# Both MLP products as seven products of block sums for eight, on 512x512 weight quarters

## Chip, cores and metric

One NeuronCore of a Trainium2 chip runs the kernel. The metric is device time in microseconds (us), lower is better, as the median of several executions. TensorE multiplies, VectorE and ScalarE read its PSUM banks and prepare operands, GpSimd does small vector work, and SyncE (SP) issues the DMA transfers.

## Reference

One inference step of a two-layer encoder over 640 token rows: 512 rows of one prompt (tiles 0 to 3 of 128 rows) and 8 streams of 16 rows (the sample tile, number 4). `D_MODEL` is 1024, `D_FF` 4096. Each layer mixes tokens (retention heads and a short convolution on a common input projection) and then applies the MLP:

```python
x = x + jnp.concatenate([ret_out, conv_out], axis=-1) @ w_out
h2 = rms_norm(x, ln2_w)
x = x + jnp.square(jax.nn.relu(h2 @ w_up)) @ w_down     # (640x1024)(1024x4096), (640x4096)(4096x1024)
```

All of it is float32. A final RMS norm gives the outputs.

## The kernel before

**Split products.** A float32 product is three passes of the TensorE format fp32r: every operand is split into a high part (ScalarE copies it into an fp32r tile) and a low part (VectorE subtracts the high part from the raw value), and high x high, high x low and low x high are accumulated in PSUM. Weights are split on the chip: a unit of 128x2048 values (1 MB) comes by DMA into `w_raw`, goes to `w_hi` on ScalarE (line 685) and to `w_lo` on VectorE (line 1046).

**Order.** Every engine has its own queue written out in program order, and semaphores count between them. In a layer come the mixer stages K, V, Q, G, C, H, B, the output projection O in two column halves of five tiles, and then the MLP. During O's second half each finished tile is normalised into `xn`, transposed by TensorE (a turn "n2": four 128x128 transposes per half; two turns, a turn pair, per tile) and split into `norm_hi` and `norm_lo`, which hold the tokens transposed (features on the partitions). Turn n2 of the last tile stands inside the first up block. The turn pair of the next layer's first norm ("n1", 0) stands inside the last down block of layer 1.

**MLP.** The hidden width is cut into 8 blocks of 512. `up_block` makes 8 groups (4 column tiles x 2 halves of 320 tokens), each 8 k-tiles x 3 passes of matmuls with 320 moving columns (line 479); ScalarE takes the relu, VectorE squares it, ScalarE and VectorE split it into `inner_hi` and `inner_lo`. `down_block` makes 10 groups (2 column halves x 5 token tiles) of 4 k-tiles x 3 passes with 512 columns (line 469), and VectorE adds each into `x` (line 1313). Up block b+1 runs before down block b, and weights have two buffers (`par`), so that splits run a whole chunk ahead. Six banks take the groups in turn.

**Engines beside TensorE.** GpSimd forms the reciprocal root of each row's mean square from ScalarE's sum of squares (line 929), which VectorE's `normalise` (line 1065) waits for.

Of the kernel before, what the change touches and what calls it, by code (L numbers as in the profile page):

```python
# [25 lines left out]
NBLK = 4 * D // 512  # L26
# [4 lines left out]
ORDER = [SAMPLE, 0, 1, 2, 3]  # L31

# [7 lines left out]
          + [("O", dh, t) for dh in range(2) for t in range(NT)])  # L40
# [3 lines left out]
                                  ("B", 0, 0), ("O", 0, 0), ("O", 1, 0))]  # L44
MIX_CHUNKS = len(STAGE_START)
UPS, DOWNS = 2 * FT, 2 * NT
PER_BLOCK = UPS + DOWNS
PER_LAYER = MIX + NBLK * PER_BLOCK
CHUNKS = MIX_CHUNKS + 2 * NBLK
# [5 lines left out]
SCALAR_PER_LAYER = len(MIX_SCALAR) + NBLK * UPS  # L55
VECTOR_PER_LAYER = len(MIX_VECTOR) + NBLK * DOWNS

# [15 lines left out]
SPLIT_TURNS = [n for n, x in enumerate(TURNS) if x[0] in ("n1", "n2", "o")]  # L73


def split_turns_to(n):
# [20 lines left out]
              **{("O", 1, t): [("n2", t - 1, 0), ("n2", t - 1, 1)] for t in range(1, NT)}}  # L97
# [3 lines left out]
def up_group(b, j):  # L101

    if isinstance(b, int) and b == 0:
        return MIX + j
    return b * PER_BLOCK + (MIX + UPS - PER_BLOCK + j)


def down_group(d, j):
    if isinstance(d, int) and d == NBLK - 1:
        return PER_LAYER - DOWNS + j  # L110
    return d * PER_BLOCK + (MIX + 2 * UPS + j)


def up_chunk(b):
    return MIX_CHUNKS if isinstance(b, int) and b == 0 else b * 2 + (MIX_CHUNKS - 1)


def down_chunk(d):
    return CHUNKS - 1 if isinstance(d, int) and d == NBLK - 1 else d * 2 + (MIX_CHUNKS + 2)


def parity_up(b_is_first):
    return MIX_CHUNKS % 2 if b_is_first else (MIX_CHUNKS + 1) % 2


def parity_down(d_is_last):
    return (CHUNKS - 1) % 2 if d_is_last else (MIX_CHUNKS + 2) % 2


def program(nc, x_p, x_s, state_ret, state_conv, norm_rows, ln2_w, w_in, conv_w, ret_w, w_out, w_up, w_down,  # L130
# [6 lines left out]
    with ctx:  # L137
# [17 lines left out]
        norm_hi = place("norm_hi", [P, KT, TOK], f32r)  # L155
        norm_lo = place("norm_lo", [P, KT, TOK], f32r)
        w_hi = place("w_hi", [P, 2, 2, 4, 512], f32r)
        w_lo = place("w_lo", [P, 2, 2, 4, 512], f32r)
        w_raw = place("w_raw", [P, 2, 4, 512], f32)


# [15 lines left out]


# [4 lines left out]
        relu = place("relu", [P, 4, HALF], f32, vo_at)  # L183
# [13 lines left out]

        norm_row = place("norm_row", [P, D], f32)
        ret_row = place("ret_row", [P, RW], f32)
        ret_state = place("ret_state", [P, H, HD], f32)  # L200
# [30 lines left out]
        mlp_bank = mix_bank + small_bank  # L231
# [23 lines left out]
        group_done = Signal("group_done", PER_LAYER, start=1)  # L255
        turned = Signal("turned", len(TURNS))
# [26 lines left out]
        squared = Signal("squared", NBLK * UPS)  # L283
        hidden_hi = Signal("hidden_hi", NBLK * UPS)
        hidden_lo = Signal("hidden_lo", NBLK * UPS)
# [34 lines left out]
        def _(sp):  # L320
            for_w_in = w_in.rearrange("l (a k p) (s c) -> l s a p k c", a=2, p=P, c=512)
            for_w_out = w_out.rearrange("l (a k p) (s c) -> l s a p k c", a=2, p=P, c=512)
            for_up = w_up.rearrange("l (a k p) (s c) -> l s a p k c", a=2, p=P, c=512)
            for_down = w_down.rearrange("l (s k p) (a c) -> l s a p k c", k=4, p=P, c=512)
# [34 lines left out]
            with sp.Fori(0, DEPTH) as layer:  # L359
# [4 lines left out]

                sp.dma_start(ret_row[:], ret_w[bass.ds(layer, 1), :].to_broadcast([P, RW])).then_inc(
# [3 lines left out]

                sp.wait_ge(group_done.sem, group_done.at(layer, 0))  # L370
# [33 lines left out]
                units(up_chunk(0), for_up, 0)  # L404
                with sp.Fori(0, NBLK // 2 - 1) as turn:
                    for b in range(2):
                        units(up_chunk(turn * 2 + (b + 1)), for_up, turn * 2 + (b + 1))
                        units(down_chunk(turn * 2 + b), for_down, turn * 2 + b)
# [271 lines left out]
        def _(act):  # L680
# [69 lines left out]
            with act.Fori(0, DEPTH) as layer:  # L750
# [6 lines left out]
                for p in range(2, NT):  # L757
                    square1(layer, p)
                    if p == NT - 1:
                        split_unit(layer, 1, 0, 1, 0)  # L760
# [668 lines left out]
```

## Time and profile before

| | |
|---|---|
| median of 3 runs | 1497.02 us (1496.27 to 1497.89) |
| profiled execution, span from its first to its last instruction | 1495.1 us |
| the same execution's own time, outside the span included | not listed apart; the three runs lie 1.2 to 2.8 us above the span |
| TensorE matmul busy | 1480.4 us (99%), 8326 instructions |
| TensorE weight loads busy | 1336.0 us (89%) |
| VectorE busy | 651.8 us (44%) |
| ScalarE busy | 393.8 us (26%) |
| GpSimd busy | 126.3 us (8%) |
| granted TensorE clock, mean | 0.998 of full speed |
| read from HBM | 115.83 MB, 82 GB/s over the span with what is written |

Busy time of TensorE is the union of overlapping matmuls, so it shows where there are gaps and not how fast the matmuls follow each other. A wait is printed in square brackets behind an instruction, with the engine that released it.

### The profile page before, as it was taken

Reading aid. Unit: us, or ns where it says so; the run is one execution under the profiler, and the core shown is the slowest. Engines: PE = TensorE matmul, PEld = TensorE weight load, DVE = VectorE, ACT = ScalarE, POOL = GpSimd, SP = SyncE. Lnnn points to the kernel's source line nnn. Section 1 sums busy time; section 2 is a strip of 40 time slices with the busy share of each in tenths; the row PEclk is TensorE's granted clock in tenths of the full one; section 3 lists DMA queues with packets and bytes.
Section 4 is the critical chain, followed back from the end, with each engine's and each line's share of the span. In section 5 each row is a group of like instructions: output and inputs, shape, how many; then the busy total and the mean of one; then the engine's idle time right before and its main releaser. Section 6 shows DMA issues by size and latency. Waiting matters only on the chain.

```text
span 1495.1 us, 21805 instructions
## 1 busy us (share of the span) xinstructions
PE 1480.4 (99%) x8326; PEld 1336.0 (89%) x8326; DVE 651.8 (44%) x970; ACT 393.8 (26%) x579; POOL 126.3 (8%) x153
## 2 busy tenths in 40 slices
PE   7999999999999999999999999999999999999998
PEld 6888999899989989989888889988999899889886
DVE  5346435355334334334362562444543433433433
ACT  5212222233123222222142203213422223223121
POOL 2343100000000000000033330000000000000000
PEclk9999999999999999999999999999999999999999
DMA  7323112122212213213042231221131221221301
GB/s 257 128 85 114 64 57 84 59 85 82 89 57 93 75 56 108 74 57 120 1 133 80 85 114 64 78 94 57 62 109 57 84 85 56 90 93 56 106 8 71
DMA packets 74643, 124.27 MB, mean 83 GB/s; under 512 B 3332, under 2 KB 20868, under 8 KB 74568
## 3 DMA queue, kind: packets, MB, share of 16 engines
q1 hardware_dynamic: 74424, 123.18, 24.9%
q8 instruction: 50, 0.82, 0.2%
q14 instruction: 25, 0.20, 0.0%
q10 hardware_dynamic: 144, 0.07, 0.0%
HBM read 115.83 MB, written 7.41 MB: 82 GB/s over the span
## 4 chain that ended last, share of the span: by engine, by line
PE 99%; DVE 0%; ACT 0%; DMA 0%; issue 0%; POOL 0%; DVEq 0%; POOLq 0%; ACTq 0%
PE bank L469 51%; PE bank L479 41%; PE bank L519 2%; PE bank L557 1%; PE bank L564 1%; PE bank L538 1%; PE bank L542 0%; PE bank L547 0%; PE bank L550 0%; DMA x<-in_x_sample 0%; PE bank L555 0%; DVE norm_lo L1089 0%; DVE w_lo L1054 0%; DVE xn L1065 0%; ACT L691 0%
## 5 line engine op out<-in xcount | busy, mean ns | idle before, releaser
L479 PE MATMUL bank<-norm_hi,w_hi 128*128 128x320 f32 x1408 | 436.1, 310 | 0.0
L479 PE MATMUL bank<-norm_hi,w_lo 128*128 128x320 f32 x1408 | 435.3, 309 | 0.0
L479 PE MATMUL bank<-norm_lo,w_hi 128*128 128x320 f32 x1408 | 435.3, 309 | 0.0
L469 PE MATMUL bank<-w_hi,inner_hi 128*128 128x512 f32 x800 | 312.1, 390 | 0.0
L469 PE MATMUL bank<-w_lo,inner_hi 128*128 128x512 f32 x800 | 311.6, 389 | 0.0
L469 PE MATMUL bank<-w_hi,inner_lo 128*128 128x512 f32 x800 | 311.5, 389 | 0.0
L685 ACT ACTIVATE w_hi<-w_raw 128x2048 fp32r<-128x2048 f32 x96 | 178.7, 1907 | 350.1 <-PE bank L469 322.4
L479 PEld LDWEIGHTS bank<-norm_hi,w_hi 128*128 128x128 f32 x1408 | 264.4, 188 | 0.6
L479 PEld LDWEIGHTS bank<-norm_lo,w_hi 128*128 128x128 f32 x1408 | 264.4, 188 | 0.5
L479 PEld LDWEIGHTS bank<-norm_hi,w_lo 128*128 128x128 f32 x1408 | 264.4, 188 | 0.0
L1313 DVE TENSOR_TENSOR x<-x,bank 128x512 f32<-128x512 f32 x180 | 123.6, 687 | 293.9 <-PE bank L469 293.9
L1046 DVE TENSOR_TENSOR w_lo<-w_raw,w_hi 128x2048 fp32r<-128x2048 f32 (+1 forms) x100 | 219.7, 2201 | 5.5 <-ACT w_hi L685 5.5
L1345 DVE TENSOR_TENSOR relu<-relu 128x320 f32<-128x320 f32 x128 | 63.0, 492 | 265.6 <-ACT relu L880 265.6
L469 PEld LDWEIGHTS bank<-w_hi,inner_lo 128*128 128x128 f32 x800 | 150.2, 188 | 31.3
L469 PEld LDWEIGHTS bank<-w_lo,inner_hi 128*128 128x128 f32 x800 | 150.2, 188 | 30.4
L469 PEld LDWEIGHTS bank<-w_hi,inner_hi 128*128 128x128 f32 x800 | 150.2, 188 | 30.4
L469 PE MATMUL bank<-w_hi,norm_hi 128*128 128x512 f32 x320 | 129.1, 404 | 2.5 <-DVE w_lo L1054 2.5
L880 ACT ACTIVATE relu<-bank 128x320 f32<-128x320 f32 x128 | 55.6, 436 | 282.5 <-PE bank L479 282.5
L469 PE MATMUL bank<-w_hi,norm_lo 128*128 128x512 f32 x320 | 125.7, 393 | 0.0
L469 PE MATMUL bank<-w_lo,norm_hi 128*128 128x512 f32 x320 | 125.5, 392 | 0.0
L926 POOL TENSOR_SCALAR var<-sums 128x1 f32<-128x1 f32 x25 | 4.8, 191 | 1196.7 <-ACT xn L703 1191.0
L469 PEld LDWEIGHTS bank<-w_hi,norm_hi 128*128 128x128 f32 x320 | 60.5, 189 | 15.2 <-ACT w_hi L691 2.9
(104 smaller groups left out, 918.1 us busy)
## 6 DMA issues: line engine op xcount, KB each, us to landing
w_raw<-in_w_mlp_up SPq DMA_DIRECT2D x32, 1024.0 KB, 5.4
w_raw<-in_w_mlp_down SPq DMA_DIRECT2D x32, 1024.0 KB, 5.0
w_raw<-in_w_in SPq DMA_DIRECT2D x28, 1024.0 KB, 5.1
w_raw<-in_w_out SPq DMA_DIRECT2D x8, 1024.0 KB, 5.0
past_state<-in_state_ret SPq DMA_DIRECT2D x8, 512.0 KB, 4.1
out_ret_s<-past_state SPq DMA_DIRECT2D x8, 512.0 KB, 4.9
x<-in_x_prompt SPq DMA_DIRECT2D x4, 512.0 KB, 12.4
norm_row<-in_norm_rows SPq DMA_DIRECT2D x3, 512.0 KB, 5.6
```

The lines of the kernel that those rows point to most:

```text
L469: mm = pe.matmul(out, act[a][:, k, tile * P:(tile + 1) * P], w_of(b, n), start=(n == 0 and m == 0), stop=(n == len(ks) - 1 and m == 2))
L479: mm = pe.matmul(out, ws[a][:, par, k // 4, k % 4, ft * P:(ft + 1) * P], norms[b][:, k, half * HALF:(half + 1) * HALF], start=(k == 0 and ...
L519: mm = pe.transpose(out[:, i * P:(i + 1) * P], src[i], identity)
L538: mm = pe.matmul(out[:, h * P:(h + 1) * P], kT[:, ORDER[p], h], qT, start=True, stop=True)
L557: mm = pe.matmul(out[:, 0:HD], q_spread[:, b], past_state[h % 2][:, b], start=False, stop=(b == NB - 1))
L564: mm = pe.matmul(out[:], k_rot[:, SAMPLE, h * HD:(h + 1) * HD], v_spread[:, 4 * c:4 * c + 4], start=True, stop=True)
L685: nc.scalar.activation(w_hi[:, par, half], w_raw[:, half], ACT.Copy).then_inc(w_hi_ready.sem, 1)
L880: nc.scalar.activation(relu[:, j % 4], mlp_bank[slot % 6][:, 0:HALF], ACT.Relu).then_inc(scalar_read.sem, 1)
L926: nc.gpsimd.tensor_scalar(tmp, src, scale, eps, ALU.mult, ALU.add).then_inc(eps_step.sem, 1)
L1046: ins = nc.vector.tensor_tensor(w_lo[:, par, half, ks], w_raw[:, half, ks], f(w_hi[:, par, half, ks]), ALU.subtract)
L1313: nc.vector.tensor_tensor(xx, xx, src[:], ALU.add).then_inc(vector_read.sem, 1)
L1345: nc.vector.tensor_tensor(relu[:, j % 4], relu[:, j % 4], relu[:, j % 4], ALU.mult).then_inc(squared.sem, 1)
```

## The change

Both MLP products are done by Strassen's method (in Winograd's form of block sums) for the four prompt tiles. The hidden width is cut into 4 blocks (`NBLK`) of 1024. A block is two quads of weights, one for up and one for down; a quad is a 1024x1024 matrix in four quarters of 512x512, named 11, 12, 21, 22. The prompt side is cut into 2x2 as well: 256 tokens x 512 features. Seven products of sums take the place of eight; the code calls them B11, B21, SUM_1112, SUM_111222, SUM_1222, B22, SUM_ALL, and the text counts them as products 1 to 7 in this order. Products 1, 2 and 6 use a quarter as it is; the other four use sums that VectorE forms in place in the raw quarters. The sample tile stays plain: it uses the four stored quarters' worth of items (products 1, 2, 5, 6: `SAMPLE_PART`) in groups of 12 matmuls with 512 columns and the tokens as the stationary operand, so its hidden values come out by rows and are turned back (`turn_sample`).

Up products have 256 moving columns, where there were 320. Weights are split by halves of an item (128x1024) into a ring of two items. The turn of tiles is ordered 0, 1, sample, 2, 3 (`OUT_ORDER`), and the last two turn pairs of a layer's norm stand inside the first up block. The differences of the normalised input are made in the first block, those of the hidden values in each block. PE here is TensorE, dve VectorE, act ScalarE.

```diff
-NBLK = 4 * D // 512
+NBLK = 4 * D // 1024
+PRODUCTS = 7
+B11, B21, SUM_1112, SUM_111222, SUM_1222, B22, SUM_ALL = range(PRODUCTS)
+SAMPLE_PART = {B11: 0, B21: 1, SUM_1222: 0, B22: 2}
...
+def half_used(item, h):
+    quad, i = divmod(item, PRODUCTS)
+    b = quad // 2
+    if quad % 2 == 0:
+        return STEP["up sample", b, i] if i in (B11, B21, B22) else STEP["up", b, i, h]
+    return STEP["down sample", b, i] if i in (B11, B21) else STEP["down", b, i, h, 1]
...
@@ SP @@
+                for quad in range(1, QUADS):
+                    first = (quad - 1) * PRODUCTS
+                    sp.wait_ge(weights_summed.sem, weights_summed.at(layer, sums_to(quad - 1, SUM_ALL, 1)))
+                    load_quarter(layer, quad, "11")
+                    sp.wait_ge(half_lo.sem, half_lo.at(layer, 2 * (first + SUM_1222) + 2))
+                    load_quarter(layer, quad, "21")
+                    sp.wait_ge(half_lo.sem, half_lo.at(layer, 2 * (first + B22) + 2))
+                    load_quarter(layer, quad, "12")
+                    sp.wait_ge(half_lo.sem, half_lo.at(layer, 2 * (first + SUM_ALL) + 2))
+                    load_quarter(layer, quad, "22")
@@ PE @@
+                def up_half(b, i, h, chain, other):
+                    item = 2 * b * PRODUCTS + i
+                    wait_item(item, h)
+                    out = {B21: other, SUM_1112: bank_c, B22: bank_c}.get(i, chain)[h]
+                    for n in range(2):
+                        cols = out[:, n * 256:(n + 1) * 256]
+                        for k in range(4):
+                            for m, (a, c) in enumerate(three):
+                                mm = pe.matmul(cols, item_half(item, h, a)[:, k, n * P:(n + 1) * P],
+                                               mlp_in[i][c][:, k], ...)
+                    mm.then_inc(step_done.sem, 1)
...
+                def up_sample(b, i):
+                    item = 2 * b * PRODUCTS + i
+                    wait_item(item, 1)
...
+                    for k in range(4):
+                        for m, (a, c) in enumerate(three):
+                            mm = pe.matmul(out, x5[a][:, k], w[c][:, :, k], ...)
...
+                def down_piece(b, i, h, pair):
+                    item = (2 * b + 1) * PRODUCTS + i
+                    wait_item(item, h)
+                    out = {B21: bank_b, SUM_1112: bank_c, B22: bank_c}.get(i, bank_a)[pair]
+                    a_item = a_ring[:, (b * PRODUCTS + i) % 2]
+                    for k in range(2):
+                        for m, (a, c) in enumerate(three):
+                            mm = pe.matmul(out[:], a_item[:, a, 2 * h + k, pair * P:(pair + 1) * P],
+                                           item_half(item, h, c)[:, k], ...)
...
+                def down(b):
+                    for i in range(PRODUCTS):
+                        if i == SUM_1222:
+                            pe.wait_ge(x_added.sem, x_added.at(layer, x_adds_to(b, B21, "sample")))
+                        if i in (SUM_1222, B22):
+                            down_sample(b, i)
...
@@ ScalarE @@
+                def weight_half(item, h):
...
+                        act.wait_ge(step_done.sem, step_done.at(layer, half_used(item - 2, h) + 1))
+                    nc.scalar.activation(item_half(item, h, 0), raw_half(quad, RAW_OF[i], h), ACT.Copy
+                                         ).then_inc(half_hi.sem, 1)
@@ VectorE, the queue of one block; lines with "if b == 0" are the first block's @@
+                def up(b):
+                    q, item = 2 * b, 2 * b * PRODUCTS
...
+                    weight_half(item + 2, 1)
+                    weight_sum(q, SUM_111222, 0)
+                    if b == 0:
+                        in_difference(0)
+                        in_difference(1)
+                    hidden_sum(b, B21, 0)
+                    weight_half(item + 3, 0)
+                    hidden_sum(b, B21, 1)
+                    weight_sum(q, SUM_111222, 1)
+                    if b == 0:
+                        in_diff_lo_of(1)
+                        in_difference(2)
+                    weight_half(item + 3, 1)
+                    weight_sum(q, SUM_1222, 0)
+                    if b == 0:
+                        in_diff_lo_of(2)
+                    weight_half(item + 4, 0)
+                    weight_sum(q, SUM_1222, 1)
+                    if b == 0:
+                        in_diff_lo_of(3)
+                        in_diff_lo_of(4)
+                    sample_lo(b, 0)
+                    weight_half(item + 4, 1)
...
+                def down(b):
+                    q, item = 2 * b + 1, (2 * b + 1) * PRODUCTS
+                    weight_sum(q, SUM_1112, 0)
+                    weight_half(item + 1, 1)
+                    a_difference(b, SUM_1112)
+                    sample_lo(b, 2)
+                    weight_half(item + 2, 0)
+                    a_difference(b, SUM_1222)
+                    for p in range(2):
+                        add_to_x(b, B11, p)
+                    weight_sum(q, SUM_1112, 1)
+                    a_item_lo(b, SUM_1112)
+                    weight_sum(q, SUM_111222, 0)
+                    weight_half(item + 2, 1)
+                    a_difference(b, SUM_111222)
+                    weight_half(item + 3, 0)
+                    for p in range(2):
+                        add_to_x(b, B21, p)
+                    add_to_x(b, B21, "sample")
+                    weight_sum(q, SUM_111222, 1)
+                    a_item_lo(b, SUM_111222)
+                    weight_half(item + 3, 1)
+                    weight_sum(q, SUM_1222, 0)
+                    a_difference(b, B22)
+                    weight_half(item + 4, 0)
+                    for p in range(2):
+                        add_to_x(b, SUM_1112, p)
+                    weight_sum(q, SUM_1222, 1)
+                    a_item_lo(b, SUM_1222)
+                    weight_half(item + 4, 1)
...
```

In the down quad the same names hold with item numbers 7 higher; the hidden values' own split items (`a_item_hi` on ScalarE, `a_item_lo` on VectorE) have a ring of two as well. The hidden values are kept in four f32 quarters, into which ScalarE copies three of the products and VectorE adds the others (`hidden_sum`), before ScalarE's relu and square.

## Rows read from the trace of the kernel before

**Rows 1.** Page, the chain that ended last: shares of the span by line.
```profile
PE bank L469 51%; PE bank L479 41%; PE bank L519 2%; PE bank L557 1%; PE bank L564 1%; PE bank L538 1%; PE bank L542 0%; PE bank L547 0%; PE bank L550 0%; DMA x<-in_x_sample 0%; PE bank L555 0%; DVE norm_lo L1089 0%; DVE w_lo L1054 0%; DVE xn L1065 0%; ACT L691 0%
```

**Rows 2.** Timeline, TensorE, 320 columns: start, duration (us), engine, line, operation, tiles, shapes.
```profile
306.55 0.31 PE L479 MATMUL bank<-norm_lo,w_hi 128*128 128x320 f32 x1
...
313.30 0.31 PE L479 MATMUL bank<-norm_hi,w_lo 128*128 128x320 f32 x1
```

**Rows 3.** Timeline, TensorE, down or O products of 512 columns.
```profile
300.31 0.40 PE L469 MATMUL bank<-w_lo,inner_hi 128*128 128x512 f32 x1
...
305.30 0.39 PE L469 MATMUL bank<-w_hi,inner_lo 128*128 128x512 f32 x1
```

**Rows 4.** Both MLPs by windows: length, busy us (instructions) by engine, clock, DMA share, GB/s.
```profile
306.32:751.23 444.91, 444.91 (x2515) 407.30 (x2514) 186.55 (x251) 114.81 (x174) 2.19 (x6) 1.00 0.22 73
1044.12:1488.12 444.00, 444.00 (x2507) 406.27 (x2505) 184.07 (x246) 113.83 (x172) 3.30 (x10) 1.00 0.21 70
```

**Rows 5.** Timeline, TensorE, transposes and plain f32 passes, and what follows each.
```profile
99.44 1.95 PE L557 MATMUL bank<-past_state,q_spread 128*128 128x128 f32 x16
...
101.22 1.88 PE L564 MATMUL bank<-v_spread,k_rot 128*128 128x512 f32 x4
...
305.53 1.03 PE L519 MATMUL bank<-const,xn 128*128 128x128 f32 x8
306.32 0.39 PE L479 MATMUL bank<-norm_hi,w_hi 128*128 128x320 f32 x1
```

**Rows 6.** Groups of instructions, shapes apart: count, busy us, mean ns, idle before.
```profile
L1065 DVE SCALAR_TENSOR_TENSOR xn<-x,rstd,norm_row 128x1024 f32<-128x1024 f32 x22 | 28.2, 1284 | 27.4 <-POOL rstd L929 27.3
...
L703 ACT ACTIVATE xn<-x 128x1024 f32<-128x1024 f32 x22 | 23.3, 1061 | 84.9 <-DVE x L1313 82.3 <-DMA x<-in_x_sample 2.6
L732 ACT ACTIVATE norm_hi<-bank 128x512 fp32r<-128x512 f32 x40 | 21.6, 589 | 38.3 <-PE bank L519 38.3
...
L1046 DVE TENSOR_TENSOR w_lo<-w_raw,w_hi 128x1024 fp32r<-128x1024 f32 x8 | 9.8, 1219 | 0.0
```

**Rows 7.** Timeline, VectorE, two instructions back to back.
```profile
758.14 1.29 DVE L1065 SCALAR_TENSOR_TENSOR xn<-x,rstd,norm_row 128x1024 f32<-128x1024 f32 x1
759.34 0.68 DVE L1106 TENSOR_TENSOR k_rot<-bank,const 128x512 f32<-128x512 f32 x1
```

**Rows 8.** Timeline, handoffs: ScalarE to VectorE, TensorE to ScalarE, VectorE to TensorE.
```profile
453.56 0.44 ACT L880 ACTIVATE relu<-bank 128x320 f32<-128x320 f32 x1 [3.06 <-PE bank L479]
...
454.03 0.49 DVE L1345 TENSOR_TENSOR relu<-relu 128x320 f32<-128x320 f32 x1 [0.81 <-ACT relu L880]
...
470.70 0.31 PE L479 MATMUL bank<-norm_hi,w_lo 128*128 128x320 f32 x1
...
471.05 0.44 ACT L880 ACTIVATE relu<-bank 128x320 f32<-128x320 f32 x1 [2.72 <-PE bank L479]
...
754.52 2.50 DVE L1054 TENSOR_TENSOR w_lo<-w_raw,w_hi 128x512 fp32r<-128x512 f32 x4 [2.40 <-ACT w_hi L691]
...
755.36 0.47 PE L469 MATMUL bank<-w_hi,norm_hi 128*128 128x512 f32 x1 [0.36 <-DVE w_lo L1054]
```

**Rows 9.** Timeline, the end: ScalarE sum, GpSimd between, VectorE.
```profile
1490.00 0.19 ACT L911 ACTIVATION_READ_ACCUMULATOR squares_out<-x 128x1 f32 x1
...
1491.23 1.42 DVE L1075 SCALAR_TENSOR_TENSOR x<-x,rstd,norm_row 128x512 f32<-128x512 f32 x2 [1.03 <-POOL rstd L929]
```

**Rows 10.** DMA issues of up weights: KB each, median us to landing.
```profile
w_raw<-in_w_mlp_up SPq DMA_DIRECT2D x32, 1024.0 KB, 5.4
```

**Rows 11.** Timeline, TensorE near the start: idle before a matmul.
```profile
12.64 0.47 PE L469 MATMUL bank<-w_hi,norm_hi 128*128 128x512 f32 x1 [2.10 <-DVE w_lo L1054]
```

**Rows 12.** Windows of 2 us at the start; the clock stands before the DMA share.
```profile
12.00:14.00 2.00, 1.36 (x5) 1.20 (x6) 2.00 (x4) 2.00 (x4) 0.00 (x0) 0.90 1.08 420
14.00:16.00 2.00, 2.00 (x6) 1.56 (x5) 0.96 (x2) 1.97 (x4) 1.44 (x3) 0.50 1.00 401
16.00:18.00 2.00, 2.00 (x12) 1.58 (x12) 2.00 (x4) 2.00 (x5) 0.20 (x1) 0.74 1.01 403
```

More of the change, by code:

```diff
@@ L96 @@
               ("B", 0, 0): [("tail",)],
[L97 to L115, printed above, removed]
@@ L118, in down_chunk @@
[L118 to L127, printed above, removed]
+              **{("O", 1, OUT_ORDER[p + 2]): [("n2", p, 0), ("n2", p, 1)] for p in range(3)}}
+PRODUCTS = 7
+B11, B21, SUM_1112, SUM_111222, SUM_1222, B22, SUM_ALL = range(PRODUCTS)
+SAMPLE_PART = {B11: 0, B21: 1, SUM_1222: 0, B22: 2}
@@ new lines, in mlp_steps @@
+def mlp_steps():
+    out = []
+    for b in range(NBLK):
+        for i in range(PRODUCTS):
+            if i == SUM_1222:
+                out.append(("up sample", b, i))
+            out.append(("up", b, i, 0))
+            if i == SUM_ALL:
+                out.append(("turn sample", b, 1))
+            out.append(("up", b, i, 1))
+            if i in (B11, B21, B22):
+                out.append(("up sample", b, i))
+            if i == SUM_1112:
+                out.append(("turn sample", b, 0))
+        for i in range(PRODUCTS):
+            if i in (SUM_1222, B22):
+                out.append(("down sample", b, i))
+            out += [("down", b, i, h, pair) for h in range(2) for pair in range(2)]
+            if i in (B11, B21):
+                out.append(("down sample", b, i))
+    return out
@@ L471, in tokens_product, with features_product @@
                 return mm
-            def features_product(out, ft, half, par, before=None):
+            def features_product(out, ft, half, chunk, before=None):
                 for k in range(KT):
@@ new lines, in up_sample @@
+                def up_sample(b, i):
+                    item = 2 * b * PRODUCTS + i
+                    wait_item(item, 1)
+                    out = sample_bank[:].rearrange("p (h c) -> p h c", h=2)
+                    w = [item_part(item, part).rearrange("p (h k c) -> p h k c", h=2, k=4) for part in range(2)]
+                    x5 = sample_in[SAMPLE_PART[i]]
+                    for k in range(4):
+                        for m, (a, c) in enumerate(three):
+                            mm = pe.matmul(out, x5[a][:, k], w[c][:, :, k],
+                                           start=(i in (B11, SUM_1222) and (k, m) == (0, 0)),
+                                           stop=(k == 3 and m == 2), skip_group_check=True)
+                    mm.then_inc(step_done.sem, 1)
@@ new lines, in down_sample @@
+                def down_sample(b, i):
+                    item = (2 * b + 1) * PRODUCTS + i
+                    wait_item(item, 1)
+                    part = SAMPLE_PART[i]
+                    pe.wait_ge(mid_lo.sem, mid_lo.at(layer, 3 * b + part + 1))
+                    for k in range(4):
+                        for m, (a, c) in enumerate(three):
+                            mm = pe.matmul(sample_bank[:], sample_mid[part][a][:, k],
+                                           item_half(item, k // 2, c)[:, k % 2],
+                                           start=(i in (B11, SUM_1222) and (k, m) == (0, 0)),
+                                           stop=(k == 3 and m == 2), skip_group_check=True)
+                    mm.then_inc(step_done.sem, 1)
@@ L1375, in _ @@
[L1375 to L1382 removed]
+                            read_turn_lo(layer, ("n2", p - 2, c))
@@ new lines, in _ @@
+                for b in range(NBLK):
+                    up(b)
+                    down(b)
+                with dve.If(layer < DEPTH - 1):
+                    split_first(layer + 1, 0)
+                for p in range(2):
+                    normalise(layer + 1, 0, p, ORDER[p], 16)
+                with dve.If(layer < DEPTH - 1):
+                    for c in range(2):
+                        read_turn_lo(layer + 1, ("n1", 0, c))
+                with dve.If(layer > DEPTH - 2):
+                    normalise_last(2)
@@ L1385, in _ @@
+                for p in range(2):
+                    add_to_x(NBLK - 1, SUM_ALL, p)
             normalise_last(3)
```

868 lines of the change are left out of this document (647 added, 221 removed).

## Prediction, made before the change was run

> **What bounds the kernel now.** I read the chain that ended last first: nearly all of it is matmuls of lines 469 and 479, so every microsecond is TensorE's, and the next question is what one matmul costs [rows 1]. A matmul's printed duration overlaps the next, so the price is start to start. At 320 columns it is (313.30 - 306.55)/46 = 0.1467 us [rows 2]; at 512 it is (305.30 - 300.31)/22 = 0.2268 us [rows 3]. Both are columns/2.4 GHz plus 13.4 ns (133.3 + 13.4; 213.3 + 13.4). The stretches by layer come next: from the first up matmul to the last down matmul 444.9 and 444.0 us, VectorE busy 187 and 184, ScalarE 115 and 114, the clock 1.00 [rows 4]. My prices give 1536 x 0.1467 + 960 x 0.2268 = 443.0 us, plus 1.0 for each turn pair, eight transposes at 0.1 and a slower matmul behind them [rows 5], of which layer 1 has two and layer 2 one: 445.0 and 444.0. So the MLPs run without a gap.
>
> **What TensorE gains.** A block is now 1024 hidden columns, four per layer. Up: 7 products x 48 matmuls of 256 columns, 4 sample groups x 12 of 512, and two sample transposes. Down: 7 x 24 and 4 x 12 of 512. The trace has no 256-column matmul. Below it stands the plain f32 pass, 128 columns with a weight load each, at (101.22 - 99.44)/16 = 0.111 us; above it the 320 columns' 0.147. I take 256/2.4 + 13.4 = 0.120, the line through both measured widths [rows 2, 3, 5]. Block: 40.3 + 10.9 + 1.0 (0.5 for four transposes and the change of width) + 38.1 + 10.9 = 101.2 us. Eight are 810; with two turn pairs in each first block and one at the first layer's end, 815. Before: 889, plus one turn pair per layer that the O stage no longer holds, 891. TensorE alone: **-76 us**.
>
> The Trainium skill (TensorE: Matmul & The Clock Gate, "Back-to-back issue gap") gives columns/2.4 + 2.5 ns, thus an estimate of 0.109 us at 256 and about 21 us less than my sum. The trace doesn't agree: the same rule gives 0.136 and 0.216 where the rows have 0.147 and 0.227 [rows 2, 3].
>
> **What VectorE and ScalarE must add.** A half item is 128x1024: VectorE 1.22 us, the next one starting 0.08 sooner, so 1.14 in a row; a 512 operation 0.68, so 0.61; a 1024 scalar_tensor_tensor 1.20; ScalarE's 1024 pass 1.05; its 512 copy 0.6 [rows 6, 7]. VectorE per block: 28 splits, 16 weight sums, 7 activation splits and 2 differences at 1.14 (60), 2 differences at 1.20 (2), 26 half-width operations (6 hidden sums, 16 adds to x, 4 for the sample) at 0.61 (16): 79 us of 101. ScalarE has 54. So neither is full on average; what counts is where the queue is full. Handoffs: 0.04 from a matmul's end to its reader (0.20 after TensorE's next start), 0.03 from ScalarE to VectorE, the same taken back, 0.15 from VectorE to a waiting matmul [rows 8].
>
> I walk one steady block (t=0 at its first matmul; products 1 to 7 in the code's order).
>
> *Stall 1, product 5 of up.* The weight ring holds two items, so item 4 may be split only when TensorE has left item 2's, its sample group included: t = 17.0 (4 x 2.88 + 2 x 2.72). Then in VectorE's order: ScalarE's half (0.20 + 1.05 + 0.03), split 1.14, hidden sum 0.61, weight sum 1.22, ScalarE 1.12, split 1.14, sum 1.22, ScalarE 1.12, split 1.14, sum 1.22, ScalarE 1.12, split 1.22, 0.15. Product 5 opens with the sample group, which needs both halves, so it starts at 30.7. TensorE needs only products 3 and 4 and a transpose, to 29.0. **1.7 us.** The sums sit between the ScalarE passes because the next half is copied out of the sum just made.
>
> *Stalls 2 and 3, products 4 and 5 of down.* From 30.7 TensorE needs 31.5 us to leave down's product 1 and its sample group: 62.2. Nothing of item 3's first half can be made earlier (same ring slot); ScalarE hands it over at 63.5. From there VectorE's queue has no gap. Ahead of product 4's activation split (a_item_lo) stand 8 operations of 1.14 (three weight splits, three weight sums, a difference, product 3's activation split), five adds to x (3.05) and a difference of 1.20; with itself (1.22) and 0.15 they end at 78.2. TensorE has done products 2 and 3 at 75.8 (5.4 + 2.7 + 5.4): **2.4 us.** Product 4 takes 5.4, to 83.6. VectorE goes on from 78.0 with a split, sum, difference (1.20), split, two adds, sum, activation split and at last the second half of product 5's weights, which its sample group wants: 5 x 1.14 + 1.20 + 2 x 0.61 + 1.22 + 0.15, thus 87.5. **3.9 us**, and 0.2 for the add to x of product 4 that still holds product 5's bank. Queued behind each are the adds to x and the splits of the next item; those keep up, being 1 us or more ahead of need. From 87.5 TensorE has 21.8 of work: the block ends at 109.5 where without waits it would at 101.3: **8.2 us each, 66 for eight**.
>
> *First block.* Five splits and three differences of the normalised input join VectorE's queue. With them the ScalarE passes of stall 1's chain find VectorE busy: from t = 20.4 it has 9 operations of 1.14 (three of them such splits), three of 0.61, one difference of 1.20 and the last split of 1.22 in a row, 14.5 us, so product 5 starts at 35.1 where TensorE, with its 2.0 of norm transposes, is ready at 31.0: 4.1 instead of 1.7, **5 us** for both layers.
>
> *End of layer 1.* The next norm's chain starts only after product 6's last piece (104.0): 0.2, ScalarE's four 512 pieces 2.2, the square 1.06 + 0.18 [rows 6, 9], 1.04 from its sum through GpSimd to VectorE's normalise [rows 9], 1.3 for that: the transposes start at 110.1 where TensorE is ready at 108.2, and with K's first product waiting 0.3 for the low part it is **2 us** in all. The end of the kernel keeps its order and its tail.
>
> *Moved or free.* Transfers: as many of 1 MB as before, landing 5.4 us after issue [rows 10]. The tightest is quarter 11 of the next up: issued after the seventh weight sum (91.8), there at 97, used at 101. It costs nothing with 4 us in hand; without them its lateness would be paid one for one, behind it quarters 21, 12 and 22 on SP's queue, the latter two needed later than the next block's start. The four quarters of the first block are queued at the O stage's second half, 30 us ahead. The mixer only has other addresses; the two splits of item 0 inside the O stage stand ahead of VectorE's add and normalise but fit a 5.4 us group.
>
> **Sum.** -76 + 66 + 5 + 2 = -3 us. The profiled execution's span is 1495.1, so 1491.8; the runs' median lies 1.9 above that span, so **1494 us**. A small difference of two large terms, then: TensorE gives back nearly all of an eighth of its products while waiting for VectorE.
>
> **Rivals.**
> 1. *The clock falls in the stalls* (slower). After 2.1 us of idle ahead of 12.64, and short ones before, the granted clock was 0.90, 0.50 and 0.74 in the next three 2 us windows, the lower level of 1.2 GHz; its price there is the missing share, 2 x (0.10 + 0.50 + 0.26) = 1.7 us [rows 11, 12]. Stall 3 is longer than that idle, and the sample group behind it is on the path. Against it: matmuls surround the stall, where the early stretch was sparse. One fall per block: +14, 1508; two, stall 2 as well: +27, 1521. Two falls in the kernel decide.
> 2. *256 columns go at 0.111* (faster): 240 of a block's 336 such matmuls are on the path (products 1, 2, 5, 6, 7; 3 and 4 hide under VectorE's chain): 8 x 240 x 0.0087 = -17: 1477. For: the f32 pass bears a weight load at that pace [rows 5]. Against: the constant 13.4 of both fp32r widths. The skill's rule above goes this way.
> 3. *The weight load is the floor at 0.147*: products 1 and 2 +2.6, 3 and 4 then longer than VectorE's chain by 0.8, 5 to 7 +3.8: 7.2 a block, +57: 1551. Against: 0.111 and the transposes' 0.1 have loads too.
> 4. *VectorE keeps ahead, no stalls in the blocks*: -76 + 2: 1423. It needs 6 us off the 24 us of queue ahead of stall 3, a quarter off each operation; the rows by form allow no such thing [rows 6].
>
> **Chances.** My forecast 0.45 (own range 1486 to 1502: the prices to 2% and the handoffs to 0.1 us), clock 0.24, pace down 0.12, pace up 0.07, no stalls 0.12 (my walk could be wrong in an order). 0.2% is 3 us, about what this measurement can tell from no change. The forecast's 0.45 splits 0.24 faster, 0.15 same, 0.06 slower: faster 0.48, same 0.15, slower 0.37. The range leaves out pace up and no stalls, 0.19: 1473 to 1521.
>
> **What the new profile would show.** 256-column matmuls 0.120 apart; TensorE idle before product 5's sample group in up (about 1.7), product 4 (2.4) and product 5's sample group in down (3.9), each released by VectorE's low parts; VectorE about 640 us busy in the MLPs, 0 idle between down's product 1 and product 5; blocks of 109 us; clock 1.00. A clock under 1.00 after stall 3, starts 0.111 or 0.147 apart, or a TensorE idle only at layer ends each name their rival. Most fragile: the walk's order of halves, since 1 us per block is 8 in the sum.

## Result, and the profile after

The changed kernel takes **1519.87 us** (median of 4 runs, 1517.21 to 1522.83) where the kernel before took 1497.45 (4 runs beside it): ratio 1.015, 95% interval 1.0132 to 1.0168, so 1.5% slower. The forecast was 1494, 0.2% faster. The four runs lie in two pairs, 1517.2 and 1517.3 against 1522.4 and 1522.8; the profile is of the first, so a difference to this kernel's median is good to some 3 us either way. The profiled execution has a span of 1515.4 us where before has 1495.1, and a mean granted clock of 0.979 where before has 0.998.

The page of the changed kernel: busy time by engine, then the chain that ended last by engine.

```profile
PE 1433.9 (95%) x8198; PEld 1265.7 (84%) x8198; DVE 947.2 (63%) x1152; ACT 593.2 (39%) x743; POOL 131.6 (9%) x153
...
PE 77%; DVE 12%; issue 6%; ACT 4%; POOL 0%; DVEq 0%; DMA 0%; ACTq 0%; POOLq 0%
```

Where [rows 1] had TensorE's two matmul lines with 92% of the chain, VectorE now holds 12% and ScalarE 4%. What TensorE waits for (total us, times, longest):

```profile
PE bank L876 <- DVE ring L1775: 25.2, 8, 3.6
PE bank L784 <- DVE ring L1775: 18.7, 8, 4.0
PE bank L863 <- DVE a_ring L1840: 17.5, 8, 2.2
```

These are the three stalls of the prediction (waits of TensorE inside a block), each eight times: L876 is product 5's sample group in down (stall 3), L784 its sample group in up (stall 1), L863 product 4 of down (stall 2), all released by VectorE. Nothing else waits inside the blocks. The price of a 256-column matmul, from the first and the last start of a product in the timeline of TensorE:

```profile
421.10 0.28 PE L770 MATMUL bank<-mlp_in_hi,ring 128*128 128x256 f32 x1
...
426.85 0.63 PE L784 MATMUL bank<-ring,sample_in_hi 128*128 128x512 f32 x2
```

Product 1 has 48 matmuls: 5.75/48 = 0.120 us each, the value taken. Now down in the second and third block, where a group's start shows the stall before it:

```profile
499.28 7.35 PE L863 MATMUL bank<-ring,a_ring 128*128 128x512 f32 x24 [2.19 <-DVE a_ring L1840]
508.56 0.74 PE L876 MATMUL bank<-ring,sample_mid_hi 128*128 128x512 f32 x2 [1.93 <-DVE ring L1775]
...
610.41 5.73 PE L863 MATMUL bank<-ring,a_ring 128*128 128x512 f32 x24 [2.19 <-DVE a_ring L1840]
619.70 1.22 PE L876 MATMUL bank<-ring,sample_mid_hi 128*128 128x512 f32 x2 [3.56 <-DVE ring L1775]
```

and the windows of the second block's stretch (the clock stands before the DMA share):

```profile
497.00:499.00 2.00, 0.09 (x1) 0.00 (x0) 2.00 (x2) 1.05 (x1) 0.00 (x0) 1.00 0.00 0
499.00:501.00 2.00, 1.72 (x5) 1.39 (x6) 2.00 (x3) 0.01 (x1) 0.00 (x0) 0.67 0.00 0
501.00:503.00 2.00, 2.00 (x7) 1.52 (x6) 1.94 (x3) 1.49 (x2) 0.00 (x0) 0.50 0.00 0
503.00:505.00 2.00, 2.00 (x10) 1.65 (x9) 2.00 (x4) 0.52 (x1) 0.00 (x0) 0.97 0.00 0
...
507.00:509.00 2.00, 0.44 (x2) 0.39 (x3) 2.00 (x3) 2.00 (x3) 0.00 (x0) 1.00 0.00 0
509.00:511.00 2.00, 2.00 (x8) 1.57 (x7) 2.00 (x3) 1.09 (x2) 0.00 (x0) 0.73 0.00 0
511.00:513.00 2.00, 2.00 (x6) 1.59 (x5) 2.00 (x3) 0.00 (x0) 0.00 (x0) 0.50 0.00 0
513.00:515.00 2.00, 2.00 (x9) 1.61 (x9) 2.00 (x3) 0.00 (x0) 0.00 (x0) 0.91 0.26 40
```

The clock goes to 0.50 (1.2 GHz) behind stall 2 and again behind stall 3, and comes back after each. The first fall costs nothing: product 4 takes 7.35 us where the third block, which has no fall there, has 5.73, and the wait behind it is 1.93 us instead of 3.56, since VectorE's low part sets the start of product 5 either way (499.28 to 508.56 is 9.28 us, 610.41 to 619.70 is 9.29). The second is paid: the 12 sample matmuls behind it take 4.18 us, where without a wait ahead of them they take 2.72. Counted in the trace, the clock falls 15 times in the two MLPs: at stall 3 in all eight blocks, at stall 1 in both first blocks and the other three of layer 2, and twice behind stall 2. Most falls begin just behind the wait, some within it. The second and third block take 111.1 and 110.8 us in layer 1 (one paid fall each) and 112.65 and 112.68 in layer 2 (two each), where the walk had 109.5.

### The profile page after: what moved, and what is told of

Same layout as the page of the kernel before. It is cut to its first block, busy times and chain, and to the rows that moved or that the text cites. A ratio compares the mean times of both kernels' runs of the same rounds, so it can differ in the third digit from the quotient of the medians.

```text
span 1515.4 us, 22275 instructions
## 1 busy us (share of the span) xinstructions
PE 1433.9 (95%) x8198; PEld 1265.7 (84%) x8198; DVE 947.2 (63%) x1152; ACT 593.2 (39%) x743; POOL 131.6 (9%) x153
## 4 chain that ended last, share of the span: by engine, by line
PE 77%; DVE 12%; issue 6%; ACT 4%; POOL 0%; DVEq 0%; DMA 0%; ACTq 0%; POOLq 0%
PE bank L612 22%; PE bank L770 15%; PE bank L622 11%; PE bank L863 11%; PE bank L784 7%; PE bank L876 5%; DVE raws L1798 4%; DVE ring L1775 3%; ACT ring L1132 3%; DVE x L1821 2%; PE bank L662 2%; DVE a_ring L1840 2%; PE bank L700 1%; PE bank L707 1%; PE bank L681 1%
## 5 line engine op out<-in xcount | busy, mean ns | idle before, releaser
L1132 ACT ACTIVATE ring<-raws 128x1024 fp32r<-128x1024 f32 x220 | 231.1, 1055 | 372.6 <-DVE raws L1798 124.3
L1775 DVE TENSOR_TENSOR ring<-raws,ring 128x1024 fp32r<-128x1024 f32 x220 | 268.8, 1222 | 169.2 <-ACT ring L1132 168.3
L863 PE MATMUL bank<-ring,a_ring 128*128 128x512 f32 x1344 | 318.1, 394 | 17.5 <-DVE a_ring L1840 17.5
L770 PE MATMUL bank<-mlp_in_hi,ring 128*128 128x256 f32 x1728 | 320.0, 283 | 0.0
L863 PEld LDWEIGHTS bank<-ring,a_ring 128*128 128x128 f32 x1344 | 254.1, 190 | 74.1 <-issue 20.8
L770 PEld LDWEIGHTS bank<-mlp_in_hi,ring 128*128 128x128 f32 x1728 | 272.1, 191 | 1.4
L770 PE MATMUL bank<-mlp_in_lo,ring 128*128 128x256 f32 x864 | 244.0, 282 | 0.0
L770 PEld LDWEIGHTS bank<-mlp_in_lo,ring 128*128 128x128 f32 x864 | 165.0, 191 | 1.4
L1798 DVE TENSOR_TENSOR raws<-raws 128x1024 f32<-128x1024 f32 x128 | 155.7, 1217 | 0.0
L622 PE MATMUL bank<-norm_hi,ring 128*128 128x320 f32 x512 | 114.5, 310 | 0.0
L876 PE MATMUL bank<-ring,sample_mid_hi 128*128 128x512 f32 x256 | 88.6, 430 | 25.2 <-DVE ring L1775 25.2
L784 PE MATMUL bank<-ring,sample_in_hi 128*128 128x512 f32 x240 | 81.8, 424 | 18.7 <-DVE ring L1775 18.7
L876 PEld LDWEIGHTS bank<-ring,sample_mid_hi 128*128 128x128 f32 x256 | 53.1, 210 | 40.4 <-DVE ring L1775 28.6
L784 PEld LDWEIGHTS bank<-ring,sample_in_hi 128*128 128x128 f32 x240 | 47.2, 206 | 29.1 <-DVE ring L1775 20.3
```

Source lines behind the costliest of these rows:

```text
L622: mm = pe.matmul(out, w_of(chunk, k // 4, a)[:, k % 4, ft * P:(ft + 1) * P], norms[b][:, k, half * HALF:(half + 1) * HALF], start=(k == 0 ...
L770: mm = pe.matmul(cols, item_half(item, h, a)[:, k, n * P:(n + 1) * P], mlp_in[i][c][:, k], start=(i in (B11, B21, SUM_1112) and (n, k, m) ...
L784: mm = pe.matmul(out, x5[a][:, k], w[c][:, :, k], start=(i in (B11, SUM_1222) and (k, m) == (0, 0)), stop=(k == 3 and m == 2), skip_group_ ...
L863: mm = pe.matmul(out[:], a_item[:, a, 2 * h + k, pair * P:(pair + 1) * P], item_half(item, h, c)[:, k], start=(i in (B11, B21, SUM_1112) a ...
L876: mm = pe.matmul(sample_bank[:], sample_mid[part][a][:, k], item_half(item, k // 2, c)[:, k % 2], start=(i in (B11, SUM_1222) and (k, m) = ...
L1132: nc.scalar.activation(item_half(item, h, 0), raw_half(quad, RAW_OF[i], h), ACT.Copy).then_inc(half_hi.sem, 1)
```

## Experiments

Before ran beside each; its medians were 1496.7 to 1497.3.

**1. Fillers in the stalls.** The waits stay, but TensorE is not idle in them: matmuls of the identity with 256 columns of a constant, into a bank that holds nothing then.

```diff
+                def fill(out, n):
+                    for _ in range(n):
+                        pe.matmul(out[:, 0:256], identity, const[:, 0:256], start=True, stop=True)
...
                         if i == SUM_1222:
                             pe.wait_ge(sample_relu.sem, ...)
+                            fill(sample_bank, 3 if b else 8)
...
+                            fill(sample_bank, 7)
+                        if i == SUM_111222:
+                            fill(back_bank, 4)
```

> Matmuls of constants (256 columns, plain f32) fill most of each TensorE wait ahead of products 4 and 5; they write banks that are free there and change no result. Theory A (the waits of 1.8, 2.2 and 3.6 us are VectorE's, and beyond them the clock falls behind them, which costs 20 us): the waits for the low parts stay where they are, the granted clock is 1.00 in the blocks, and the time falls by 20 us to 1500. Theory B (the lower clock costs nothing because TensorE waits anyway): clock 1.00 but the time stays at 1520 within 2.

Measured: 1498.91 us (10 runs), ratio to before 1.0016 (1.0006 to 1.0025), clock 0.997. TensorE's idle time shrinks to half a microsecond a stall, while VectorE's parts arrive when they did (the start of up's product 4 and that of the sample group behind it lie 7.68 us apart in both kernels):

```profile
PE bank L881 <- DVE ring L1783: 4.3, 8, 0.6
PE bank L788 <- DVE ring L1783: 4.0, 8, 0.6
PE bank L868 <- DVE a_ring L1848: 3.7, 8, 0.5
```

A steady block is 109.75 us, the walk's 109.5 nearly. With the same stalls and the clock held, 21.0 us of the changed kernel's 1519.9 are gone (18 to 24 over its own spread): **that is the clock's price**. What is left is 1.9 us above before, so even with the clock held the change gains nothing. The forecast of 1500 for this run was met.

**2. Without the weight sums.** The 16 sums of a block handle one column instead of 1024, which leaves the block sums of the weights out.

```diff
-                    nc.vector.tensor_tensor(out, out, raw_half(quad, b, h), ALU.add)...
+                    nc.vector.tensor_tensor(out[:, 0, 0:1], out[:, 0, 0:1], raw_half(quad, b, h)[:, 0, 0:1], ALU.add)...
```

> Leaves out the weight sums on VectorE but for one column each, with every count kept, so the products are of wrong quarters; all other work is as in the changed kernel. Theory A (VectorE's queue ahead of three points sets the waits, and TensorE's own work is 76 us less than before): the waits at product 5 of up and product 4 of down vanish, about 1 us stays at product 5 of down, the clock stays up, time 1434. Theory B (256-column matmuls or other things cost more than counted and VectorE is not the cause): 1480 or more.

Measured: 1446.39 us (4 runs), ratio 0.966 (0.9644 to 0.9676), clock 0.999; stall 2 gone, stall 1 gone but for 1.1 us in both first blocks, stall 3 down to this, at which the clock falls nowhere:

```profile
PE bank L876 <- DVE ring L1775: 11.5, 8, 1.5
```

So VectorE's work is what the stalls are made of. The block is 103.3 us: 101.1 of matmuls, the price I had given for TensorE alone (101.2), and 2.0 to 2.2 at stall 3 from start to start (1.4 of it shown as idle), twice what I had expected. That doubling (8 us) and the two ends (1.9 and 2.4, below) are the 12 us by which it stays above the 1434 expected.

**3. Two operations moved in down.** The weight sum (SUM_1112, 1) and the difference for SUM_1222 go ahead of the first split of product 3's weights, behind which VectorE's gapless run began.

```diff
-                    weight_half(item + 2, 0)
+                    weight_sum(q, SUM_1112, 1)
                     a_difference(b, SUM_1222)
+                    weight_half(item + 2, 0)
                     for p in range(2):
                         add_to_x(b, B11, p)
-                    weight_sum(q, SUM_1112, 1)
```

> Only VectorE's order in down changes: the second half of product 3's weight sum and the difference for product 5 stand ahead of the split that waits for TensorE, in the idle 1.5 us. Theory A: the wait at product 4 of down falls from 2.2 to about 0.6, the one at product 5 stays 3.6, so 1.6 us per block, 13 in all: 1507, with the clock still falling behind the third wait. Theory B (the queue is not what counts but the chain through ScalarE): no change, 1520.

Measured: 1516.02 us (4 runs, 1510.6 to 1518.3), ratio 1.0121 (1.0096 to 1.0147), clock 0.977. That is a miss by 9 us, and with the changed kernel's own spread hardly a gain. Stall 2 fell from 2.19 to 1.21 only, since now VectorE ran out of ready work and waited for ScalarE's half, and stall 3 stayed at 3.6:

```profile
491.25 1.22 DVE L1852 SCALAR_TENSOR_TENSOR diff<-diff,hidden 128x1024 f32<-128x1024 f32 x1
493.02 1.23 DVE L1775 TENSOR_TENSOR ring<-raws,ring 128x1024 fp32r<-128x1024 f32 x1 [0.54 <-ACT ring L1132]
```

Steady blocks are 110.1 and 110.3 us in layer 1 (1.0 and 0.5 less) and 112.6 in layer 2 (0.1 less). In layer 2 the lower clock ate the gain: the fall at stall 3 lasted longer, and the sample group behind it took 5.29 us, where the changed kernel has 4.44. A shift of two operations isn't a cure while stall 3 and the falls stay.

**4. A quarter of the sums on GpSimd.** Those of SUM_1222 go there, behind a semaphore of their own.

```diff
+                for quad in range(QUADS):
...
+                    for h in range(2):
+                        pool.wait_ge(weights_summed.sem, weights_summed.at(layer, sums_to(quad, SUM_1112, h)))
+                        settle(pool)
+                        out = raw_half(quad, "12", h)
+                        nc.gpsimd.tensor_tensor(out, out, raw_half(quad, "22", h), ALU.add
+                                                ).then_inc(pool_summed.sem, 1)
...
-                    weight_sum(q, SUM_1222, 0)
...
-                    weight_sum(q, SUM_1222, 1)
```

> The weight sums of product 5 (two halves per quad, 16 quads in all) go to GpSimd, which is idle there. Theory A (VectorE's queue): the wait in up vanishes but in the first block, the third one falls from 3.6 to about 1.3, the second stays, 36 us less of waits and fewer falls of the clock: about 1469. Theory B (GpSimd and VectorE hinder each other, as GpSimd's small operations took 1.2 us instead of 0.2 beside VectorE): VectorE's operations get longer or the sums come late, 1495 or more.

Measured: 1492.08 us (6 runs), ratio 0.9964 (0.9952 to 0.9977), clock 0.978: 23 above theory A and 3 below theory B's bound, whose mechanism is what the trace shows. Stalls 1 and 3 are gone from the steady blocks, but stall 2 grew to 3.5 us, with a fall of the clock in all eight blocks, and product 3 got a new wait of 1.2. Both engines in the timeline, GpSimd's rows first:

```profile
425.63 2.38 POOL L1471 TENSOR_TENSOR raws<-raws 128x1024 f32<-128x1024 f32 x1 [1.26 <-DVE raws L1810]
...
476.13 3.20 POOL L1471 TENSOR_TENSOR raws<-raws 128x1024 f32<-128x1024 f32 x1 [48.12 <-DVE raws L1810]
485.81 3.21 POOL L1471 TENSOR_TENSOR raws<-raws 128x1024 f32<-128x1024 f32 x1 [6.47 <-DVE raws L1810]
```
```profile
477.01 3.42 DVE L1859 TENSOR_TENSOR diff<-hidden 128x1024 f32<-128x1024 f32 x1
...
486.68 3.42 DVE L1810 TENSOR_TENSOR raws<-raws 128x1024 f32<-128x1024 f32 x1
```

A VectorE operation with two inputs in SBUF that starts beside GpSimd's takes 3.42 us instead of 1.22, and ends 1.1 us after GpSimd's has ended (479.33 to 480.43): it waited. GpSimd waits too: its sum takes 2.4 us where VectorE is idle (six of them, as at 425.63), and 3.2 where it starts within a VectorE operation of this kind. So a sum moved to GpSimd took 1.14 us off VectorE's queue and could put 2.2 us on it, in down just ahead of product 4. The Trainium skill (SBUF — State Buffer, "SBUF: two separate sides") names the mechanism: the two engines' shared ports are a lock held for a whole instruction, and a VectorE operation with both inputs in SBUF takes part in it. The trace agrees, with these 3.42 us for 1.22; VectorE operations of 512 columns with one input in PSUM took their usual 0.68 us beside the same sum (at 312.9 and 313.5).

**5. VectorE's queue in another order.** No operation is added or taken away. Both halves of the 12+22 sum are made early in each pass where VectorE was idle; halves are split in pairs, so that ScalarE's pass of one runs beside VectorE's split of the other; what product 5 doesn't need goes behind its weights. ScalarE's queue in down follows (activation parts behind the weight halves).

```diff
                     weight_sum(q, SUM_1112, 1)
+                    weight_sum(q, SUM_1222, 0)
+                    weight_sum(q, SUM_1222, 1)
...
                     weight_half(item + 3, 0)
+                    weight_half(item + 3, 1)
...
                     a_item_lo(b, SUM_111222)
-                    weight_half(item + 3, 1)
-                    weight_sum(q, SUM_1222, 0)
-                    a_difference(b, B22)
                     weight_half(item + 4, 0)
+                    weight_half(item + 4, 1)
                     for p in range(2):
                         add_to_x(b, SUM_1112, p)
-                    weight_sum(q, SUM_1222, 1)
                     a_item_lo(b, SUM_1222)
-                    weight_half(item + 4, 1)
+                    a_difference(b, B22)
```

> The same operations as the changed kernel, issued in another order on VectorE (and in down on ScalarE): both halves of the 12+22 weight sum are made right behind those of 11+12 while VectorE is idle early in each pass, both halves of an item are split in a row, and in down what product 5 doesn't need (its activation split, the next difference, the adds to x of product 3) goes behind product 5's weight splits. Theory A (the three stalls are VectorE's queue at those places, each also letting the clock fall; neither VectorE nor ScalarE is short of time over a block): stalls 1 to 3 go to 0.3 us or less each, with them 60 us of waiting and the 20 us of clock, new small waits of up to 0.5 us a block at down's product 4: span 1515 - 80 + 4 = 1439, median 1441, clock 0.998. Rival B (the two engines' queues are full where it matters, so work moved behind a stall comes back as a wait at products 6 and 7 or at the next block's start): 3 to 5 us a block return, 1475 to 1500, and with clock falls up to 1515. Rival C (the weight load floors a 256-column matmul when nothing waits): 1495 and more.

Measured: 1483.28 us (4 runs), ratio 0.9912 (0.9895 to 0.9928), clock 0.983. Stalls 1 and 3 are gone, stall 2 has become the only one, 4.0 us long:

```profile
PE bank L863 <- DVE a_ring L1840: 31.8, 8, 4.0
```

The forecast of 1441 was missed by 42 us. The time lies in rival B's range, but the work did not come back where it said (products 6, 7 or the next block): the rest of the queue's backlog had gathered at product 4, and the clock fell there in all eight blocks.

**6. Fillers at stall 3 alone**, in the changed kernel: `fill(sample_bank, 7)` of the first run, the other two left out.

> The changed kernel with the fillers of the first run at one place only: seven 256-column matmuls on a constant into the sample bank ahead of product 5's sample group in down (stall 3); stalls 1 and 2 are left idle. Theory A (a fall of the clock belongs to the wait just before it): the eight falls behind stall 3 go, of which about seven were on the path at 1.5 to 1.7 us, those behind stall 1 stay: median 1507, clock 0.985 to 0.99. Rival B (the clock falls by the idle time of a block as a whole): it stays at 1516 to 1520 with falls at other places. Rival C (one wait starts it and the others only keep it low): all falls but those of the first blocks go, 1501.

Measured: 1505.59 us (4 runs), ratio 1.006 (1.0043 to 1.0077), clock 0.990. The falls behind stall 3 are gone; six are left in the trace, behind stall 1 of both first blocks (4.0 us) and behind four of the fourteen other waits of 1.8 and 2.2 us. So a fall belongs mostly to the wait at which it comes, and the forecast of 1507 was met: stall 3's falls cost 14.3 us of the 21.0 by the medians (12 to 17 over the changed kernel's spread). Which of the waits of 1.8 and 2.2 us are followed by a fall differs from the changed kernel's trace; what decides that stays open.

**7. A better order.** On top of run 5: product 2's three adds to x go behind product 5's weight splits, and ScalarE makes the second half of down's first item ahead of its squares.

```diff
                     weight_half(item + 7, 0)
+                    weight_half(item + 7, 1)
                     sample_square(b, 1)
                     square_hidden(b, h12, B22, -1.0)
-                    weight_half(item + 7, 1)
...
-                    for p in range(2):
-                        add_to_x(b, B21, p)
-                    add_to_x(b, B21, "sample")
                     weight_half(item + 3, 0)
                     weight_half(item + 3, 1)
                     a_item_lo(b, SUM_111222)
                     weight_half(item + 4, 0)
                     weight_half(item + 4, 1)
+                    for p in range(2):
+                        add_to_x(b, B21, p)
+                    add_to_x(b, B21, "sample")
```

> The re-ordered kernel of the fifth run, whose one remaining wait is 3.98 us at down's product 4, with two more moves: the three adds of product 2 to x go from ahead of product 4's activation split to behind product 5's weight splits (1.87 us off the queue), and on ScalarE the second half of down's first item goes ahead of the sample's and the hidden quarter's squares, so that VectorE's run without a gap, which began at 576.7 behind a wait of 2.91 us for it, begins some 2 us sooner. Theory A (only VectorE's queue there sets the wait, and the clock falls only behind it): the wait goes to 0.1 to 0.5 us and all falls with it: span 1480.6 - 8 x 3.6 - 18 = 1434, median 1436, clock 0.998. Rival B (the moved adds and splits return as a wait of 1 to 2 us at product 5's sample group or at product 6): 1445 to 1455. Rival C (the squares that go back delay product 2's activation split): a new wait of 1 us at down's product 2, 1444 and more.

Measured: **1447.03 us** (5 runs), ratio **0.9666** (0.9653 to 0.9679), faster than both kernels. Its page and its waits:

```profile
PE 1408.4 (97%) x8198; PEld 1249.0 (86%) x8198; DVE 943.8 (65%) x1152; ACT 594.9 (41%) x743; POOL 131.1 (9%) x153
```
```profile
PE bank L863 <- DVE a_ring L1840: 8.2, 8, 1.0
...
PE bank L792 <- ACT sample_hidden L1182: 4.3, 10, 0.5
```

A wait of 1.0 us is left before product 4 and 0.5 before a transpose, and the clock stays at 1.00 through both MLPs:

```profile
304.66:725.00 420.34, 410.27 (x2457) 364.72 (x2456) 334.53 (x344) 215.79 (x254) 3.26 (x6) 1.00 0.23 77
1018.28:1436.00 417.72, 409.16 (x2449) 363.93 (x2448) 332.55 (x339) 213.88 (x250) 5.05 (x8) 1.00 0.22 75
```

Its steady block is 103.1 us, against 110.8 to 112.7, with the same 1152 instructions on VectorE. The forecast was 1436: the wait before product 4 stayed above the 0.1 to 0.5 us it gave, and the one before the transpose was in none of its theories. From start to start the two cost 2.0 us a block.

**8. Fillers ahead of product 4 in run 5's kernel**, eight of them (`if i == SUM_111222: fill(back_bank, 8)`).

> The re-ordered kernel of the fifth run with eight filler matmuls of 256 columns on a constant ahead of down's product 4, where its one wait of 3.98 us a block stands. Theory A (product 4, which took 3.0 and 1.7 us longer behind that wait than its 5.44, does so by the clock alone): 8 x 2.3 = 18 us less, 1465, clock 0.997, the wait's total of VectorE unchanged under the fillers. Rival B (it is longer because its own operands come late, piece by piece): no more than 3 us less, 1480.

Measured: 1465.53 us (4 runs), ratio 0.9788 (0.9773 to 0.9803), clock 0.997: 17.8 less than run 5, as forecast, by the clock alone: 2.2 us for each of its eight stalls on average (2.8 and 1.6 in the second and third block).

## Why the prediction was wrong

The step that failed is the term for the clock, which the sum put at nothing; the rest of the sum was right to 6 us. 1519.9 lies outside the forecast's own range of 1486 to 1502, and in the wide one (1473 to 1521) only through rival 1.

*TensorE alone, -76:* right. 256 columns go at 0.120 us, the matmuls of a block take 101.1 us for the 101.2 computed, so rivals 2 and 3 (0.111 and 0.147 us a matmul) are out.

*Stalls of a steady block, 1.7, 2.4 and 3.9 plus 0.2:* right. From start to start they are 1.93 (up's product 4 with the wait behind it, 7.67 us less 5.74), 2.35 (7.79 less 5.44) and 3.85 (9.29 less 5.44), 8.1 in sum for 8.2. VectorE's run without a gap ahead of them stands in the timeline as walked (the first row waits for ScalarE's half; from there 19 groups with none):

```profile
484.62 1.23 DVE L1775 TENSOR_TENSOR ring<-raws,ring 128x1024 fp32r<-128x1024 f32 x1 [1.53 <-ACT ring L1132]
485.76 1.22 DVE L1849 TENSOR_TENSOR hidden<-hidden 128x1024 f32<-128x1024 f32 x1
...
507.28 1.23 DVE L1775 TENSOR_TENSOR ring<-raws,ring 128x1024 fp32r<-128x1024 f32 x1
```

Run 2 showed that the sums are a necessary part of it, runs 5 and 7 that their place in the queue is what counts. The first block's stall 1 was 4.0 for 4.1. VectorE was busy 334 us in each MLP, 669 for the 640 forecast, which moved no stall.

*The clock:* here it failed. The sum took 1.00 throughout, and the case in which it falls had 0.24, on the argument "matmuls surround the stall, where the early stretch was sparse". The runs say that this does not protect: the clock fell at every wait of 3.5 us and more in the changed kernel and in run 5, with TensorE full before and after, at waits of 1.8 to 2.2 us in some blocks, and at waits of 1.5 us and less in none (runs 2 and 7). Rival 1 was worked out at 14 us for one fall a block and 27 for two, 1.7 each from [rows 12]; there were 15 falls, two of them hidden in a later wait, and run 1 measured 21.0 us for them. That rival 1's time of 1521 came so exactly is in part luck: it had 6 us more for the clock, and the two ends and the blocks, below, made up 6 that it lacked. The Trainium skill (TensorE: Matmul & The Clock Gate, "What's actually happening") has the clock set by how busy TensorE has been recently. The runs agree: with fillers in the same waits (run 1) there was no fall in the MLPs, without them 15.

*End of layer 1, 2 us:* about 1.9 too low, read in the trace only. TensorE waits 1.80 us for the normalised rows, as forecast, and 1.90 before K's first product, where the prediction had 0.3; no run shows what the second is made of. *"The end of the kernel keeps its order and its tail":* wrong by 2.4. From TensorE's end the tail takes 9.2 us (1506.2 to 1515.4), where before it was 6.8 (1488.3 to 1495.1):

```profile
1503.36 1.28 DVE L1499 SCALAR_TENSOR_TENSOR xn<-x,rstd,norm_row 128x1024 f32<-128x1024 f32 x1 [0.71 <-POOL rstd L1362]
1503.41 1.29 POOL L1359 TENSOR_SCALAR var<-sums 128x1 f32<-128x1 f32 x1
...
1505.36 1.28 DVE L1509 SCALAR_TENSOR_TENSOR x<-x,rstd,norm_row 128x1024 f32<-128x1024 f32 x1 [0.71 <-POOL rstd L1362]
1506.56 1.28 DVE L1821 TENSOR_TENSOR x<-x,bank 128x512 f32<-128x512 f32 x2
...
1509.65 1.14 POOL L1359 TENSOR_SCALAR var<-sums 128x1 f32<-128x1 f32 x1 [0.23 <-ACT squares_out L1344]
```

GpSimd's operation on one element a row takes 1.29 us beside VectorE's normalise instead of 0.19; two such delays (1501.48 and 1503.41) hold back the normalise at 1505.36, behind which the last two adds to x stand in VectorE's queue, and a third (1509.65) holds back the last normalise itself by 0.95. In before none of GpSimd's 25 such operations was delayed. This is the reading of the timeline with what run 4 showed of the two engines; no run took it apart.

In sum: 1494.0, and 21.0 for the clock, 1.9 and 2.4 for the two ends, 1.5 for six steady blocks at 109.75 instead of 109.5, make 1520.8 for 1519.9 measured. The clock's term is shown by run 1; the ends are read from the trace, and no run took them away.

*Rival 4, "no stalls, 1423":* its condition was put wrongly. I asked for operations a quarter shorter; what it takes is 6 us of the 24 ahead of stall 3 at another place of the queue, and they fit. Run 7 is that case, with 2.0 us a block above TensorE's 101.1, two small waits in each first block and the longer ends: 1447.

## What to carry to other kernels

Where a change makes the bounding engine faster, its gain can hang on re-ordering the feeding engine's queue to the new pace. Here the busy share said little (VectorE was 63% busy), and the order ahead of each handoff was worth 73 us (1519.9 to 1447.0). Walk the queue, and where the walk gives a wait, first ask which of the operations ahead of it nobody needs yet. Add the fall of the clock to the price of a wait on TensorE: here some 1.6 us (changed kernel) to 2.2 us (run 5) each on average, for nearly every wait of 3.5 us or more and some of 1.8 to 2.2, unless a later wait swallows it. One run with fillers in the waits shows how large that loss is.

## What the runs showed of the hardware

Inside the MLP blocks of the changed kernel and of runs 3 to 6 the clock fell at 35 of 36 waits of 3.5 to 4.0 us (the exception is the third block's stall 3 in run 3) and at 16 of 38 waits of 1.8 to 2.2 us, each between full stretches of matmuls; at none of 92 waits of 0.5 to 1.5 us (runs 1 to 8). A fall ahead of another wait for a different engine cost nothing (9.28 and 9.29 us). A VectorE operation with two inputs in SBUF and a GpSimd operation that reads SBUF waited for each other's end: 3.42 us for 1.22 on VectorE, 1.29 for 0.19 and 3.2 for 2.4 on GpSimd. A 128x1024 f32 add takes GpSimd 2.4 us undisturbed, VectorE 1.22.
